# A decoder layer with expert retrieval on one core: one query-weight chunk kept on chip in place of two, and eleven places for gathered rows in place of ten

## Chip, cores, metric

The kernel runs on one core of a Trainium2 chip. The metric is the device time of one execution in microseconds (us). Of the kernel before there are three timed runs: 3097.0, 3091.28 and 3106.02 us, median 3097.0 us. Everything is float32.

## What is computed

The reference is one decoder layer over 1024 tokens of width 1024. Cut to what matters here:

```python
mix = hybrid_mixer(h, ...)      # x @ w_in; window attention and a gated DeltaNet; then @ w_out
h   = layer_norm(ALPHA * h + mix)
# PEER: product-key retrieval over 128*128 experts, in blocks of 128 tokens
q   = (xb @ w_query).reshape(L, 8, 2, 128)               # 2048 query columns
s   = einsum('lhpd,hpkd->lhpk', q, sub_keys)             # 16 lists of 128 scores
vals, idx = top_k(s, 16)                                 # for each list
best, pos = top_k(all 16*16 sums, 16); expert = ...      # 8 heads x 16 experts for a token
gate = softmax(best)
u, v = expert_u[expert], expert_v[expert]                # 1024 + 1024 numbers each
hid  = gelu(einsum('ld,lhkd->lhk', xb, u))
out  = einsum('lhk,lhkd->ld', hid * gate, v)
h    = layer_norm(ALPHA * h + out)
```

Each token draws 128 experts of its own and each expert is a row of 2048 numbers (u and v side by side), so the layer reads 1024 x 128 rows of 8 KB, 1073.7 MB, whatever is done about the weights.

## The kernel before, in words

The 1024 tokens are eight blocks (n = 0 to 7) of 128, one token in each partition. Two jobs are interleaved. The **mix** of block n is the projections, attention, DeltaNet, output projection, first norm, the queries of PEER and the choice of experts. The **experts** of block n are 128 slots: slot j is one gather of 128 rows (1 MB, an indirect DMA that POOL issues at L541), a dot product with the token's x on DVE (`experts`, L1849), a gelu and a gate on ACT (L1329 to L1336, which makes a small diagonal matrix `diag`), and four matmuls on PE that add the weighted v rows into `expert_sum` (L1007). While the mix of block n runs, the last slots of block n-1 are consumed. How much goes where is written out by hand: `EARLIER` and `OWN` (L146 to L158) give for each named step of the mix how many pairs of slots DVE, ACT and PE take after it. The steps of the choice of experts are `top0`, `more0`, `sel0`, `rest0`, `pick0` for the first two heads, then the same with 1, 2, 3. `pick0` writes the first 32 slots' indices (`expert_used`, L1799 and L1829) and raises `staged`. POOL waits for it (L533) before gather 0 of the new block. That moment is called the **turnover** here. Block n-1's slots 126 and 127 are dotted right after `pick0` (mark `pick0`, L1800), slots 124 and 125 after `rest0`, 122 and 123 after `sel0`. Then `turn_over` reads `expert_sum` on DVE (L1867) and copies x (L1838), and the steps from `top1` on keep DVE busy.

**The ring.** Gathered rows lie in `ring`, RING = 10 places of 8 KB per partition (1 MB each in all). `place(n, j)` is place (128 n + j) mod RING. POOL issues gather j when the slot RING before it has been added by PE:

```python
pool.wait_ge(*added.at(n, j - RING + 1))     # L536
gather(n, j)
```

**The weights.** `w_in`, `w_out` and `w_query` are cut into 23 chunks of 256 columns, 1 MB each: 0 to 10 for the input projection, 11 to 14 for the output projection, 15 to 22 for the queries. There are two staging buffers, `chunk0` and `chunk1`, each used as two halves of 512 KB. SP issues the loads in the order of use (`load`, L491 to L500). The load of a half waits until PE has used the half four loads earlier:

```python
sp.wait_ge(half_used, HALF_USED[last[0], last[1], last[2]])    # last = LOADS[g - 4]
alone(sp)
sp.dma_start(half_place(g), ...).then_inc(half_in[g % 4], 16)
```

The chunks in `KEPT`, 17 and 20 (the third and the sixth query chunk), are loaded once and stay in `kept` for all eight blocks; they are skipped at L523. So SP loads 4 + 6 chunks for the output projection and the queries of a block, and the input projection's chunks once for two blocks. The loads of x (`load_xT`, L505) stand behind the query chunks in SP's order, and behind them the chunks of the next blocks' input projection.

**The query phase on PE** (L952 to L987): `query_chunks(i)` multiplies chunks 15+2i and 16+2i, 32 matmuls each (L614), `score_keys(i)` makes four lists of scores (L967), and between them stand matmuls of pairs of slots of the block before: chunks 15, 16, scores, 17, 18, pair, scores, pair, 19, 20, pair, scores, pair, 21, 22, pair. PE takes a pair one pair later than DVE.

**Block 0.** Its weights are loaded ahead into the chunk buffers and the ring, which holds no rows yet: `EARLY` = 2 + RING places, used round (`early_place`, L446). The first gathers wait until PE has used the chunk in their place (L549).

Of the kernel before, what the change touches and what calls it, by code (L numbers as in the profile page):

```python
# [46 lines left out]
IN_CHUNKS = (HEADS * HD + 2 * KV * HD + 4 * DH * DK) // W  # L47
OUT_CHUNKS = D // W
Q_CHUNKS = LISTS * P // W
CHUNKS = IN_CHUNKS + OUT_CHUNKS + Q_CHUNKS  # L50
RING = 10
PAIRS = SLOTS // 2
SPAN = P // 2
PART = SLOTS // 4
DIAGS = 4
KEPT = (IN_CHUNKS + OUT_CHUNKS + 2, IN_CHUNKS + OUT_CHUNKS + 5)
STREAMED = [c for c in range(CHUNKS) if c not in KEPT]
EARLY = 2 + RING * 2 * D // (KT * W)

# [6 lines left out]
def in_pass(n):  # L66

    two = [m for m in (n + 1, n + 2) if m < NB]
    kinds = [(kind, two, PASS_BANKS[t]) for t, kind in enumerate(FLAT_KINDS if n % 2 else CONV_KINDS)] if two else []
    if n == 0:  # L70
        kinds += [(kind, [1], (b,)) for kind, b in zip(FLAT_KINDS, (5, 3, 4))]
    return kinds
# [7 lines left out]
def _use(c, blocks, streamed, halves=(0, 1)):  # L80
    for half in halves:
        if streamed:
            LOADS.append((c, blocks[-1], half))
    for m in blocks:
        for half in halves:
            HALF_USED[c, m, half] = len(HALF_USED) + 1
            if streamed:
                LOAD_OF[c, m, half] = len(LOADS) - len(halves) + halves.index(half)
# [6 lines left out]
for _n in range(NB):  # L95
# [4 lines left out]
    for _c in range(IN_CHUNKS + OUT_CHUNKS, CHUNKS):  # L100
        _use(_c, [_n], _n > 0 and _c not in KEPT)
    for _kind, _blocks, _ in in_pass(_n):
# [90 lines left out]
def build(nc, io):  # L193
    ctx = ExitStack()
    with ctx:
        def sb(name, cols, dt=F32, parts=P):
            return ctx.enter_context(nc.sbuf_tensor(name, [parts, cols], dt))

        def sem(name):
            return ctx.enter_context(nc.semaphore(name))  # L200

        def signal(name, per_block=1, before=0):
            return Signal(sem(name), per_block, before)
# [27 lines left out]
        chunk = [sb(f"chunk{i}", KT * W) for i in range(2)]  # L231
        ring = sb("ring", RING * 2 * D)
        kept = sb("kept", len(KEPT) * KT * W)

# [48 lines left out]
        late_in = sem("late_in")  # L283
        kept_in = [sem(f"kept_in{i}") for i in range(len(KEPT))]
        early_in = [sem(f"early_in{i}") for i in range(EARLY)]
# [86 lines left out]
        late_gates = signal("late_gates", 1)  # L372
        gathered = [sem(f"gathered{i}") for i in range(RING)]
        dotted = signal("dotted", SLOTS)
# [3 lines left out]
        diag_ready = signal("diag_ready", SLOTS)  # L378
        added = signal("added", SLOTS, before=RING)
        sums_read = signal("sums_read", 1, before=1)  # L380
# [18 lines left out]
        def place(n, j):  # L399

            r = (n * SLOTS + j) % RING
            return ring[:, r * 2 * D:(r + 1) * 2 * D]

        def arrived(n, j):

            return gathered[(n * SLOTS + j) % RING], 16 * ((n * SLOTS + j) // RING + 1)

# [34 lines left out]
        def kept_chunk(c):  # L442
            i = KEPT.index(c)
            return kept[:, i * KT * W:(i + 1) * KT * W]
# [29 lines left out]
        def _(sp):  # L474
# [5 lines left out]
            for c in range(1, CHUNKS):  # L480
                if c == IN_CHUNKS:
                    sp.dma_start(x1[:, :], io["x"][0]).then_inc(x_loaded.sem, 16)
                if c in KEPT:
                    sp.dma_start(kept_chunk(c), io["weights"][c]).then_inc(kept_in[KEPT.index(c)], 16)
# [1469 lines left out]
```

## Time and profile before

| | us |
|---|---|
| median of three runs (lowest, highest) | 3097.0 (3091.28, 3106.02) |
| profiled execution, its own time | 3092.87 |
| its span, first to last instruction | 3091.0 |
| PE busy in the span | 2352.3 (76%) |
| DVE busy | 2239.9 (72%) |
| POOL busy | 1195.2 (39%) |
| ACT busy | 1121.6 (36%) |
| data moved by the DMA engines | 1235.90 MB, mean 400 GB/s |

The profile is that of one execution, whose time is 4.1 us below the median. 1.9 us lie outside its span. Engines: PE is the matrix engine (PEld its weight loads), DVE the vector engine, ACT the scalar engine, POOL the engine that issues the gathers, SP the one that issues the weight loads. "DMA share" is the mean busy share of the 16 DMA engines. It reads up to 1.02 where they are all busy, so it can't tell full from nearly full, and GB/s beside it does. A line number is one of the code above.

### The profile page before, as it was taken

Reading aid. Unit: us, or ns where it says so; the run is one execution under the profiler, and the core shown is the slowest. Engines: PE = TensorE matmul, PEld = TensorE weight load, DVE = VectorE, ACT = ScalarE, POOL = GpSimd, SP = SyncE. Lnnn points to the kernel's source line nnn. Section 1 sums busy time; section 2 is a strip of 40 time slices with the busy share of each in tenths; the row PEclk is TensorE's granted clock in tenths of the full one; section 3 lists DMA queues with packets and bytes.
Section 4 is the critical chain, followed back from the end, with each engine's and each line's share of the span. In section 5 each row is a group of like instructions: output and inputs, shape, how many; then the busy total and the mean of one; then the engine's idle time right before and its main releaser. Section 6 shows DMA issues by size and latency. Waiting matters only on the chain.

```text
span 3091.0 us, 37872 instructions
## 1 busy us (share of the span) xinstructions
PE 2352.3 (76%) x11842; PEld 1330.6 (43%) x11842; DVE 2239.9 (72%) x5638; ACT 1121.6 (36%) x3530; POOL 1195.2 (39%) x1028
## 2 busy tenths in 40 slices
PE   8996878868788677877779778886778767785654
PEld 7773435424356343544346343542435434351111
DVE  5488656986679766897658966699657986678645
ACT  4123533254333533235322353224432363323222
POOL 0034452344423454234533345234443344434442
PEclk9998999989899898988989889988988889887777
DMA  8199999999999999999999999999999999999997
GB/s 350 42 383 412 420 421 406 412 413 420 420 408 418 417 420 420 397 407 419 420 419 404 416 420 421 407 399 413 420 420 404 418 418 420 420 372 421 410 421 323
DMA packets 189000, 1235.90 MB, mean 400 GB/s; under 512 B 21752, under 2 KB 21880, under 8 KB 54656
## 3 DMA queue, kind: packets, MB, share of 16 engines
q0 software_dynamic: 147456, 1073.81, 84.0%
q1 hardware_dynamic: 39168, 154.32, 12.7%
q10 hardware_dynamic: 2176, 5.36, 0.4%
q8 instruction: 95, 1.56, 0.2%
q14 instruction: 105, 0.86, 0.1%
HBM read 1229.21 MB, written 4.19 MB: 399 GB/s over the span
## 4 chain that ended last, share of the span: by engine, by line
DVE 32%; PE 29%; DMA 25%; ACT 6%; issue 5%; POOL 2%; DVEq 0%; POOLq 0%; SPq 0%; ACTq 0%
DMA ring<-in_uv,expert_used 24%; DVE ring L1849 14%; PE expert_sum L1007 13%; PE bank L614 7%; PE bank L621 2%; PE bank L603 2%; ACT diag L1336 2%; POOL ring L541 2%; DVE arena L1477 2%; DMA chunk<-in_weights 1%; DVE conv L1497 1%; DVE arena L1792 1%; DVE arena L1789 1%; DVE arena L1492 1%; DVE arena L1486 1%
## 5 line engine op out<-in xcount | busy, mean ns | idle before, releaser
L541 POOL DMA_INDIRECT ring<-in_uv,expert_used x1024 | 1195.0, 1167 | 1863.2 <-PE expert_sum L1007 1413.1
L1007 PE MATMUL expert_sum<-ring,diag 128*64 128x512 f32 x4096 | 1185.8, 708 | 639.1 <-ACT diag L1336 638.1
L1849 DVE CUSTOM_DVE_ANT_0 ring<-ring,x_pair 128x1024 f32<-128x1024 f32 x1024 | 1227.6, 1223 | 478.6 <-DMA ring<-in_uv,expert_used 472.8
L1007 PEld LDWEIGHTS expert_sum<-ring,diag 128*64 128x64 f32 x4096 | 312.3, 155 | 1261.0 <-issue 1246.4
L1329 ACT ACTIVATE h_raw<-h_raw 128x2 f32<-128x2 f32 x512 | 104.1, 203 | 1457.5 <-DVE h_raw L1849 1456.4
L1336 ACT ACTIVATE diag<-const,h_raw 128x64 f32<-128x64 f32 x1024 | 292.6, 332 | 4.9 <-PE expert_sum L1007 4.9
L1332 ACT ACTIVATE h_raw<-h_raw,gate_used 128x1 f32<-128x1 f32 x1024 | 245.6, 286 | 16.8
L614 PEld LDWEIGHTS bank<-oT,chunk 128*128 128x128 f32 x1344 | 152.7, 192 | 22.7 <-issue 22.7
L614 PE MATMUL bank<-oT,chunk 128*128 128x128 f32 x1344 | 158.6, 277 | 0.0
L1477 DVE MAX8 arena<-arena 128x8 f32<-128x128 f32 (+1 forms) x384 | 103.7, 325 | 32.6 <-ACT arena L1282 27.3
L603 PE MATMUL bank<-chunk,oT 128*128 128x256 f32 x464 | 110.0, 388 | 0.0
L603 PEld LDWEIGHTS bank<-chunk,oT 128*128 128x128 f32 x464 | 85.7, 191 | 41.1 <-issue 30.7
L614 PEld LDWEIGHTS bank<-o_cat,chunk 128*128 128x128 f32 x768 | 92.2, 200 | 21.2 <-issue 20.7
L621 PEld LDWEIGHTS bank<-arena 128*128 128x128 f32 x640 | 80.7, 202 | 41.4 <-issue 37.9
L614 PE MATMUL bank<-o_cat,chunk 128*128 128x128 f32 x768 | 96.8, 286 | 0.1
L1329 ACT ACT_TABLE_LOAD x74 | 94.9, 1283 | 5.2 <-DVE h_raw L1849 3.9
L621 PE MATMUL bank<-arena 128*128 128x128 f32 x640 | 90.5, 294 | 2.0 <-ACT arena L1236 0.6
L1849 DVE DVE_READ_ACCUMULATOR2_ANT h_raw<- 128x1 f32 x1024 | 83.9, 82 | 0.0
L1278 ACT COPY arena<-bank 128x512 f32<-128x512 f32 x32 | 18.7, 585 | 176.7 <-PE bank L614 176.7
L595 PE MATMUL bank<-chunk,o_cat 128*128 128x256 f32 x320 | 76.9, 392 | 7.2 <-DMA chunk<-in_weights 7.0
L1497 DVE SCALAR_TENSOR_TENSOR conv<-conv_in,conv_w,conv 128x128 f32<-128x128 f32 x288 | 77.8, 344 | 0.0
L614 PEld LDWEIGHTS bank<-xT_even,chunk 128*128 128x128 f32 x576 | 67.4, 196 | 13.7 <-issue 13.7
(276 smaller groups left out, 2621.6 us busy)
## 6 DMA issues: line engine op xcount, KB each, us to landing
chunk<-in_weights SPq DMA_DIRECT2D x228, 512.0 KB, 8.2
ring<-in_weights SPq DMA_DIRECT2D x17, 1024.0 KB, 23.9
ring<-in_uv,expert_used POOLq DMA_INDIRECT x1024, 15.5
chunk<-in_weights SPq DMA_DIRECT2D x4, 1024.0 KB, 20.4
x<-in_x SPq DMA_DIRECT2D x8, 512.0 KB, 14.6
out<-oT ACTq DMA_DIRECT2D x8, 512.0 KB, 9.2
o_cat<-in_xT SPq DMA_DIRECT2D x7, 512.0 KB, 14.6
xT_even<-in_xT SPq DMA_DIRECT2D x4, 512.0 KB, 10.0
```

The source lines that it names most:

```text
L541: pool.indirect_dma_start(out=place(n, j), out_offset=None, in_=io["uv"], in_offset=bass.IndirectOffsetOnAxis(ap=expert_used[:, j:j + 1], ...
L595: mm = pe.matmul(out, act[:, k, :], w[:, k % 4, :], start=(k == 0), stop=(k == KT - 1))
L603: mm = pe.matmul(out, act[:, k, :], w[:, k % 4, :], start=(k == ks[0]), stop=(k == ks[-1]))
L614: mm = pe.matmul(out, w[:, k % 4, i * P:(i + 1) * P], act[:, k, :], start=(k == 0), stop=(k == KT - 1))
L621: mm = pe.matmul(out[:, hs], lhsT[:, hs], rhs[:, hs], start=True, stop=True)
L1007: mm = pe.matmul(expert_sum[i][c * SPAN:(c + 1) * SPAN, :], diag[:, (j % DIAGS) * SPAN:(j % DIAGS + 1) * SPAN], place(n, j)[:, D + i * 512 ...
L1329: act.activation(h_raw[:, pair[0]:pair[1] + 1], h_raw[:, pair[0]:pair[1] + 1], ACT.Gelu).then_inc(gelued.sem, 1)
L1332: act.activation(h_raw[:, j:j + 1], h_raw[:, j:j + 1], ACT.Copy, scale=gate_used[:, j:j + 1]).then_inc(weighted.sem, 1)
L1336: act.activation(diag[:, (j % DIAGS) * SPAN:(j % DIAGS + 1) * SPAN], C["halves"], ACT.Copy, scale=h_raw[:, j:j + 1]).then_inc(diag_ready.s ...
L1477: ins = dve.max(values[:, one[part]], one[2])
L1497: stt(out=convo[:, t, :], in0=conv3[n % 2][:, t, k:k + P], scalar=conv_w[:, t * TAPS + k:t * TAPS + k + 1], in1=convo[:, t, :], op0=ALU.mu ...
L1849: dve.tensor_tensor_reduce(u, u, x_pair[:, (j % 2) * D:(j % 2 + 1) * D], 1.0, 0.0, ALU.mult, ALU.add, h_raw[:, j:j + 1]).then_inc(dotted.s ...
```

## The change

`KEPT` holds chunk 18 alone (the fourth query chunk). Chunks 17 and 20 are now streamed through the staging buffers for each block, and `kept` is half as large (8 KB less per partition). `RING` is 11, one place of 8 KB more per partition. `STREAMED` has 22 chunks in place of 21 and `EARLY` is 13 in place of 12. Nothing else in the file changes; the waits follow from these constants.

```diff
-RING = 10
+RING = 11
 PAIRS = SLOTS // 2
 SPAN = P // 2
 PART = SLOTS // 4
 DIAGS = 4
-KEPT = (IN_CHUNKS + OUT_CHUNKS + 2, IN_CHUNKS + OUT_CHUNKS + 5)
+KEPT = (IN_CHUNKS + OUT_CHUNKS + 3,)
 STREAMED = [c for c in range(CHUNKS) if c not in KEPT]
 EARLY = 2 + RING * 2 * D // (KT * W)
```

## Rows read from the trace of the kernel before

**Rows 1.** The page: GB/s in 40 slices of the span, and the two queues.

```profile
GB/s 350 42 383 412 420 421 406 412 413 420 420 408 418 417 420 420 397 407 419 420 419 404 416 420 421 407 399 413 420 420 404 418 418 420 420 372 421 410 421 323
...
q0 software_dynamic: 147456, 1073.81, 84.0%
q1 hardware_dynamic: 39168, 154.32, 12.7%
```

**Rows 2.** The page: the chain that ended last, by engine.

```profile
DVE 32%; PE 29%; DMA 25%; ACT 6%; issue 5%; POOL 2%; DVEq 0%; POOLq 0%; SPq 0%; ACTq 0%
```

**Rows 3.** Busy time by windows: stretch, its length, engines, granted clock, DMA share, GB/s.

```profile
664.00:860.00 196.00, 149.66 (x675) 74.61 (x676) 128.40 (x244) 85.29 (x268) 89.02 (x75) 0.86 1.01 420
176.00:3072.00 2896.00, 2191.01 (x10799) 1196.18 (x10799) 2138.04 (x5342) 1061.40 (x3401) 1181.92 (x1013) 0.88 1.01 414
```

**Rows 4.** The same view: the seven turnovers, blocks 1 to 7.

```profile
536.00:546.00 10.00, 7.74 (x30) 3.09 (x26) 6.82 (x19) 2.76 (x7) 6.63 (x7) 0.97 0.91 322
900.00:912.00 12.00, 11.37 (x63) 6.63 (x61) 8.75 (x22) 3.75 (x10) 6.07 (x7) 1.00 0.95 352
1264.00:1280.00 16.00, 13.87 (x96) 9.81 (x93) 10.05 (x29) 6.17 (x15) 4.26 (x5) 1.00 0.88 315
1640.00:1650.00 10.00, 9.69 (x37) 3.94 (x35) 6.87 (x16) 3.50 (x8) 7.03 (x8) 0.89 0.97 349
2002.00:2014.00 12.00, 10.89 (x84) 8.97 (x86) 9.55 (x28) 6.17 (x15) 2.90 (x3) 1.00 0.87 292
2376.00:2384.00 8.00, 7.68 (x43) 4.17 (x42) 4.71 (x14) 3.50 (x8) 4.91 (x5) 1.00 0.90 311
2738.00:2750.00 12.00, 11.68 (x89) 8.95 (x87) 9.53 (x28) 6.17 (x15) 2.85 (x3) 1.00 0.36 133
```

**Rows 5.** DVE in order of time at block 2's turnover: start, length, idle before.

```profile
896.26 1.22 DVE L1849 CUSTOM_DVE_ANT_0 ring<-ring,x_pair 128x1024 f32<-128x1024 f32 x1 [3.52 <-DMA ring<-in_uv,expert_used]
...
902.48 0.72 DVE L1829 CAST expert_used<-arena 64x16 uint32<-64x16 f32 x4
```

**Rows 6.** POOL in order of time, same turnover.

```profile
883.49 0.93 POOL L541 DMA_INDIRECT ring<-in_uv,expert_used  x1 [0.30 <-issue]
904.10 1.17 POOL L541 DMA_INDIRECT ring<-in_uv,expert_used  x1 [19.68 <-DVE expert_used L1829]
```

**Rows 7.** PE and SP in order of time, same turnover: chunks 17, 19, 21 and 22, loads.

```profile
871.65 3.84 PE L614 MATMUL bank<-oT,kept 128*128 128x128 f32 x32
883.82 3.84 PE L614 MATMUL bank<-oT,chunk 128*128 128x128 f32 x32
895.98 7.41 PE L614 MATMUL bank<-oT,chunk 128*128 128x128 f32 x64
...
861.59 26.49 SPq L500 DMA_DIRECT2D chunk<-in_weights  x8
```

**Rows 8.** DMA of 860 to 896 us: its queues, and the chunk loads to landing.

```profile
q0 software_dynamic: 1510, 11.01, 73.9%
q1 hardware_dynamic: 1077, 3.95, 27.3%
...
chunk<-in_weights SPq DMA_DIRECT2D x8, 512.0 KB, 9.1
```

**Rows 9.** Source line 500 over the whole span: its loads to landing.

```profile
DMA to landing us min/median/max: 3.8/8.2/12.9
```

**Rows 10.** By windows again: dips outside the turnovers.

```profile
256.00:272.00 16.00, 10.41 (x47) 4.61 (x47) 13.21 (x43) 10.59 (x28) 6.80 (x6) 1.00 0.97 386
596.00:668.00 72.00, 52.62 (x211) 26.81 (x211) 69.84 (x206) 25.93 (x84) 28.85 (x25) 0.84 1.00 407
1328.00:1400.00 72.00, 54.39 (x230) 28.83 (x228) 69.56 (x205) 26.21 (x84) 29.62 (x26) 0.87 1.01 407
2060.00:2144.00 84.00, 65.91 (x278) 35.01 (x274) 81.38 (x242) 29.70 (x99) 33.81 (x30) 0.87 1.00 402
2912.00:2924.00 12.00, 12.00 (x33) 3.63 (x33) 5.75 (x11) 2.54 (x10) 3.09 (x5) 0.62 0.88 344
```

## The prediction

> **What bounds the kernel now.** I read the 40 slices and the queues first. From the sixth slice on the core moves 397 to 422 GB/s in every slice but three, and the gathers' queue alone takes 84.0% of the 16 DMA engines' time, the weights' queue 12.7% [rows 1]. No compute engine comes near that: PE is at 76%, DVE at 72%. The chain of waits seems to say otherwise, DVE 32%, PE 29%, DMA 25% [rows 2], but it follows semaphores, and a gather that queues behind others is late because of bytes, whoever issued it. So the deciding view is busy time by windows. Between 664 and 860 us the DMA moves 420 GB/s without a break; I take 420 as full. From 176 to 3072 us it averages 414 [rows 3], which is 2896 x 6/420 = 41 us short of full. Time is therefore bytes over 420, plus at most those 41 us, plus the start and the tail, which the change hardly touches. The question is how many bytes come on top, and whether they fall into the 41 us.
>
> Where do the 41 us lie? Mostly at the seven turnovers [rows 4]. Their shortfalls against 420, window by window, are 2.3, 1.9, 4.0, 1.7, 3.7, 2.1 and 8.2 us, together 23.9. The mechanism is in DVE's and POOL's order of time. Slot 125's row is there at 896.26, DVE then runs the index work of pick0 and writes the indices at 902.48 [rows 5], and POOL, which has issued the last gather of the old block at 883.49, sits 19.68 us and issues the next at 904.10 [rows 6]. From 896 the DMA has only slots 126 and 127 and some weights left. A second group of dips lies where DVE is 96 to 98% busy with the choice of experts, and at one place in block 7 where PE is held up [rows 10]: 1.3, 2.2, 2.2, 3.6 and 2.2 us, 11.5 together. There the ring is full of rows that nobody has consumed yet.
>
> **Bytes added.** One more chunk is streamed in blocks 1 to 7: 7 x 2 halves of 0.524 MB = 7.34 MB. Price: the weights' queue moved 154.32 MB in 12.7% of 3091 us, 393 GB/s [rows 1]. That gives **+18.7 us** if nothing hides it. Startup is even: 23 chunks are loaded once before and after, and 13 early places with 1 kept chunk hold as many as 12 with 2. The one kept load less and one ring load more cancel. SP's 14 added issues cost nothing: SP has no other work, and in the phase in question it waits for PE.
>
> The Trainium skill, page DMA: Bandwidth & Descriptors, section Bandwidth, measured 341 GB/s for a 1 MB transfer against 425 for 16 MB, and gives as a rule to batch to 1 MB and more. At that page's 341 the added bytes would be 21.5 us, an estimate. The trace doesn't agree for this kernel, since with both queues at work it moves 414 to 417.
>
> **Where the bytes fall.** SP is paced by PE: a half is loaded when the half four loads back is used. Before, from 861.59, SP loads 18, 19, 21, 22 and then x. After, it loads 17, 19, 20, 21, 22 and then x, with 22 issued when PE has used chunk 20 (some 890.3 to 891.2) and not chunk 19 (886.6 to 887.5). Everything behind it moves back by 3.7 us, towards or into the gap that opens at 896. Two bounds. Above, all bytes go ahead of slot 125 and nothing is hidden, 0 us. Below, each turnover swallows what it has room for, at most one chunk's 2.67 us (18.7/7): 2.3 + 1.9 + 2.67 + 1.7 + 2.67 + 2.1 + 2.67 = 16.0 us. Which is nearer? From 860 to 896 the weights' queue got 27.3% of the DMA, 3.95 MB or 110 GB/s [rows 8], with loads outstanding nearly all the time. The new order wants 3.67 MB in the 34.4 us up to 896, 107 GB/s. So the queue already moved about what the new order asks of it, little is taken from the gathers, and the excess slides behind slot 125. I take two thirds of 16.0: **-10.7 us**.
>
> By the Trainium skill, same page, section Queues, rings and completion order, each DMA engine round-robins between the queues that have work, a packet from each. By that rule the weights' share isn't changed by how deep either queue is, and nearly all 16.0 us would be hidden. A share near 27% fits it, but no row here has the deeper queue.
>
> **The eleventh place.** POOL may run one gather further ahead, 1.05 MB or 2.5 us of DMA work. Where the DMA is full anyway this is worth nothing. Before pick0 it is worth nothing either, as the gathers' queue isn't empty there. It counts where the DMA runs dry because the ring is full, once a block: after a turnover POOL issues 11 gathers in a burst and not 10, and DVE starts its long busy stretch with 2.5 us more in stock. Each dip can give back at most 2.5 us: 1.3 + 2.2 + 2.2 + 2.5 + 2.2 = 10.4 [rows 10]. Below that, an odd ring splits the pairs: PE frees two places at a time, and only the even slot of a pair is asked for a pair earlier. Bounds 0 and 10.4; I take **-6.5 us**. If the dips are really DVE being late, the place moves the DMA's idle time rather than removing it.
>
> **Waits on PE.** Chunk 17 was on chip; now its first half is issued at 861.59 and wanted at 871.65 [rows 7], 10.1 us later, against 9.1 us to landing in this phase [rows 8]. Chunk 21, issued at about 886.6 and wanted at 895.98, has 9.4; chunk 22, issued at 890.3 and wanted at 899.7, has 9.4. All three are covered by under 1.1 us, and the longest landing in the trace is 12.9 [rows 9]. Queued behind a late chunk on PE are the pairs of slots, the scores, and the last pair of the block, for which DVE's turn_over waits; then top1 and all of DVE's busy stretch start late, and there DVE has no slack. Bounds: 0, and 12.9 - 9.4 = 3.5 us in each of seven turnovers, 24.5. I take half a microsecond in each: **+3.5 us**.
>
> Chunk 18, now kept, leaves an equal pause in SP's order where 17 and 20 had theirs. DVE, ACT and the arithmetic are unchanged.
>
> **Sum.** 18.7 - 10.7 - 6.5 + 3.5 = +5.0 us. On the profiled execution's 3092.9 that is 3097.9; that execution lies 4.1 us below the median of the three, so against the median it is 3102. I write 3100.
>
> **Rivals.** A change under 0.5%, 15.5 us, can hardly be told from none here.
>
> *All hidden.* The gaps take 16.0, the place gives 10.4, PE never waits: 18.7 - 26.4 = -7.7, 3085 on the profiled time, 3089 on the median. For it speak the 107 against 110 GB/s. Against it, two turnovers have room for under 2 us. Chance 0.2. To go past -15.5 the kernel would have to lose 34 of its 41 us of shortfall while it moves more bytes: 3077. Only a ring that shrinks the turnover gap itself does that, by slot 125 being there earlier. Its gather has 22 us between issue and arrival, all of it queueing, so issuing it earlier brings it no earlier. Chance 0.06.
>
> *Bytes in full.* The weights push slot 125 back, pick0 with it, and the gap is as wide as before: 18.7 less a few us of the ring, 3109 to 3116. For it speaks that the DMA is full up to 896, so what is added before that has to displace something. Chance 0.14.
>
> *PE starved of chunks 17, 21 and 22.* On the slower side, and it decides once a half takes longer than the 10.1 or 9.4 us it has. Five chunks in a row on a queue that gets 110 GB/s need 5.24/110 = 47.6 us, and 22 is wanted after 39. If 3.5 us are lost at each turnover and DVE's busy stretch passes them on: 18.7 - 10.7 - 6.5 + 24.5 = +26, 3119 to 3123. Against it: from 896 on the gathers are nearly done and the weights have the DMA for themselves. Chance 0.12.
>
> That the change doesn't do what it says is no rival: 8 KB per partition go from one buffer to the other, and both constants are used throughout.
>
> **The numbers.** The forecast (partly hidden, 3092 to 3108) has 0.48. Faster by over 0.5%: 0.06. Slower by over 0.5% (above 3112.5): 0.12 from the starved PE and a bit over half of "bytes in full", 0.08, so 0.20. Within 0.5%: 0.74. The range reaches down to the all-hidden case, 3083, and up to the starved one, 3121.
>
> **What would show it.** Bytes 7.34 MB more, at 242 chunk loads in place of 228. The seven turnover windows nearer to 420 GB/s than in [rows 4], with block 7's 8.2 us cut by some 2.5. The dips of [rows 10] shallower. PE's waits for chunks in the query phase under a microsecond each. POOL's burst after a turnover with 11 gathers. It is wrong if slot 125 arrives 2.5 us later after chunk 15 than now with the turnover windows unchanged, if L614 waits for chunks by several us at each turnover, or if the dips of the DVE-bound stretches stay as deep as they are.

## The result and the profile after

The changed kernel takes 3126.7 us in the median of six runs (3120.6 to 3135.1), the one before 3099.5 us beside it. The ratio is 1.0086, interval 1.0072 to 1.0100: 27 us slower, 22 to 31, where 5 were forecast and 3121 was the upper end. The experiments come in four later sets, each taken together on one chip with the kernel before beside it: e1 to e4, e5 to e8, e9 to e12, e13 to e15. The changed kernel, run again in three of them, gave 24.5, 13.3 and 29.7 us. The sign is sure, the size is one of 13 to 30 us, and what makes it vary is part of the findings. All costs below are (ratio - 1) x 3097 us; two executions far off all others, 4467 us in e2 and 3494 us of the kernel before beside e1 to e4, are left out of the ratios.

The page of the changed kernel, its GB/s in 40 slices, its queues, and from its costliest groups the query matmuls and the reading of the sums; it answers to [rows 1]. Its span is 3118.7 us; this execution, of 3120.56 us, was the fastest of the six, so the profile shows 27.7 us more than before.

```profile
GB/s 347 41 394 415 420 420 399 406 415 410 420 414 398 418 414 420 402 408 415 421 419 406 417 413 421 412 393 413 420 420 407 405 417 420 420 374 419 421 421 311
...
q0 software_dynamic: 147456, 1073.81, 83.5%
q1 hardware_dynamic: 41184, 161.66, 13.1%
...
L614 PE MATMUL bank<-oT,chunk 128*128 128x128 f32 x1568 | 198.3, 286 | 27.7 <-DMA chunk<-in_weights 27.6
L614 PEld LDWEIGHTS bank<-oT,chunk 128*128 128x128 f32 x1568 | 187.1, 198 | 60.5 <-DMA chunk<-in_weights 32.9
...
L1867 DVE SCALAR_TENSOR_TENSOR oT<-x_pair,expert_sum 64x512 f32<-64x512 f32 x32 | 21.9, 685 | 85.5 <-remote 42.9
```

The bytes are as foreseen: the weights' queue has 161.66 - 154.32 = 7.34 MB more, in 242 chunk loads, for 0.4% more of the engines' time. What is new stands in the last three rows. PE, which before waited 0.4 us in all for chunks at L614, waits 27.6 us, 3.9 at each turnover. And DVE waits 85.5 us for the sums at L1867 over its eight readings, where it waited 24.6. ("Remote" is the profile's word for a releaser that it couldn't name; the program has one core, and the wait at that line is for PE.)

DVE and then POOL in order of time, changed kernel, the turnover of block 2, as [rows 5, 6]:

```profile
905.30 0.72 DVE L1829 CAST expert_used<-arena 64x16 uint32<-64x16 f32 x4
...
924.10 1.39 DVE L1867 SCALAR_TENSOR_TENSOR oT<-x_pair,expert_sum 64x512 f32<-64x512 f32 x2 [15.14 <-PE expert_sum L1007]
```

```profile
906.93 1.17 POOL L541 DMA_INDIRECT ring<-in_uv,expert_used  x1 [16.55 <-DVE expert_used L1829]
...
914.62 0.94 POOL L541 DMA_INDIRECT ring<-in_uv,expert_used  x1 [0.30 <-issue]
918.02 0.94 POOL L541 DMA_INDIRECT ring<-in_uv,expert_used  x1 [2.46 <-PE expert_sum L1007]
```

From the indices to the reading of the sums 18.8 us pass; before it was 6.6 (902.48 to 909.07):

```profile
909.07 2.78 DVE L1867 SCALAR_TENSOR_TENSOR oT<-x_pair,expert_sum 64x512 f32<-64x512 f32 x4 [2.93 <-PE expert_sum L1007]
```

POOL's burst, which was to be eleven gathers long, stops after seven, because the places wait for PE. The reason is in PE's order of time over the same stretch, as [rows 7]:

```profile
875.61 1.16 PE L614 MATMUL bank<-oT,chunk 128*128 128x128 f32 x8
878.62 4.57 PE L614 MATMUL bank<-oT,chunk 128*128 128x128 f32 x24 [1.85 <-DMA chunk<-in_weights]
883.01 3.75 PE L614 MATMUL bank<-oT,kept 128*128 128x128 f32 x32
...
903.68 1.16 PE L614 MATMUL bank<-oT,chunk 128*128 128x128 f32 x8
906.69 8.15 PE L614 MATMUL bank<-oT,chunk 128*128 128x128 f32 x56 [1.85 <-DMA chunk<-in_weights]
```

PE starts chunk 17 with the half that is there, and stands still until the second half lands; the same at chunk 21. And there is a second loss: the 24 records after the first stop take 4.57 us where 32 on the kept chunk take 3.75. The windows show why; columns are length, engines, granted clock, DMA share, GB/s. First the changed kernel, then the same kernel in e9:

```profile
878.00:883.00 5.00, 4.38 (x24) 4.38 (x25) 4.47 (x18) 0.00 (x0) 0.66 (x1) 0.66 1.00 411
...
907.00:915.00 8.00, 8.00 (x58) 7.84 (x58) 1.89 (x7) 0.00 (x0) 6.17 (x7) 0.79 1.00 395
```

```profile
875.50:879.00 3.50, 3.14 (x28) 3.14 (x29) 2.72 (x7) 0.00 (x0) 0.76 (x1) 1.00 1.00 411
...
903.00:907.00 4.00, 3.18 (x28) 2.99 (x28) 3.83 (x12) 0.00 (x0) 0.34 (x1) 1.00 0.81 293
```

PE had stood still for 1.85 us each time, and then the granted clock was 0.66 over 5 us: part of them at the lower of its two levels, 1.2 GHz, where in the kernel before it was 1.00, that is 2.4 GHz, from 864 to 909. In e9 PE stood still at the same two places, for 1.5 and 2.3 us, and the clock stayed at 1.00; the 24 records after the first stop took 2.94 us. So the fall doesn't follow from the length of one stop, and what decides it these rows don't show.

**Where the DMA's shortfall went.** The prediction's account was bytes plus shortfall. The shortfall against 420 GB/s in us, summed over windows of 2 us (one above 420 counts against it), for three parts of each block counted from the reading of the sums (R): turnover, R - 20 to R + 15; busy stretch, R + 15 to R + 130; the rest.

| kernel | turnovers | busy stretches | rest |
|---|---|---|---|
| before | 26.6 | 10.8 | 0.4 |
| changed | 19.5 | 24.0 | 4.9 |
| e9, changed | 30.0 | 8.8 | 0.5 |
| e13, changed | 19.0 | 24.3 | 8.1 |
| e2, bytes at the turnover | 11.6 | 27.3 | 0.4 |
| e4, third staging buffer | 13.6 | 22.4 | 0.6 |
| e3, idle matmuls | 38.3 | 35.9 | 0.7 |
| e7, twelve places alone | 35.9 | 1.0 | 0.3 |
| e8, nine places, three chunks kept | 37.2 | 44.2 | 5.6 |

In the first set and in e13 the turnovers did fill, as foreseen, and what was filled there opened again in the busy stretch behind it. In e9 neither happened: the same kernel had 30.0 us at the turnovers, more than the kernel before, and 8.8 behind them. The busy stretches of blocks 1 and 2, windows of the kernel before and of the changed one:

```profile
557.00:672.00 115.00, 88.92 (x378) 49.27 (x374) 111.07 (x338) 39.74 (x134) 42.83 (x38) 0.89 1.01 412
924.00:1039.00 115.00, 90.51 (x536) 56.81 (x532) 109.56 (x333) 39.03 (x129) 40.87 (x38) 0.89 1.01 417
```

```profile
564.00:679.00 115.00, 86.83 (x378) 48.63 (x375) 111.17 (x339) 39.82 (x135) 42.68 (x39) 0.90 1.01 406
939.00:1054.00 115.00, 88.02 (x538) 55.98 (x536) 110.87 (x336) 40.56 (x133) 42.51 (x39) 0.92 1.00 404
```

### The profile page after: what moved, and what is told of

It is laid out like the page before. It is cut to its first block, busy times and chain, and to the rows that moved or that the text cites. A ratio compares the mean times of both kernels' runs of the same rounds, so it can differ in the third digit from the quotient of the medians.

```text
span 3118.7 us, 37900 instructions
## 1 busy us (share of the span) xinstructions
PE 2354.9 (76%) x11842; PEld 1333.6 (43%) x11842; DVE 2233.6 (72%) x5638; ACT 1121.8 (36%) x3530; POOL 1202.6 (39%) x1028
## 3 DMA queue, kind: packets, MB, share of 16 engines
q1 hardware_dynamic: 41184, 161.66, 13.1%
## 4 chain that ended last, share of the span: by engine, by line
DVE 35%; DMA 26%; PE 23%; ACT 6%; issue 6%; another core or an unknown queue 3%; POOL 1%; DVEq 0%; POOLq 0%; SPq 0%; ACTq 0%
DMA ring<-in_uv,expert_used 22%; DVE ring L1849 15%; PE expert_sum L1007 10%; PE bank L614 5%; DMA chunk<-in_weights 4%; DVE arena L1477 2%; ACT diag L1336 2%; PE bank L603 2%; PE bank L621 1%; DVE arena L1492 1%; DVE conv L1497 1%; DVE arena L1486 1%; DVE arena L1484 1%; POOL ring L541 1%
## 5 line engine op out<-in xcount | busy, mean ns | idle before, releaser
L1007 PE MATMUL expert_sum<-ring,diag 128*64 128x512 f32 x4096 | 1180.5, 705 | 626.4 <-ACT diag L1336 624.4
L1007 PEld LDWEIGHTS expert_sum<-ring,diag 128*64 128x64 f32 x4096 | 311.6, 154 | 1244.5 <-issue 1229.8
L1332 ACT ACTIVATE h_raw<-h_raw,gate_used 128x1 f32<-128x1 f32 x1024 | 245.7, 287 | 16.8
L614 PE MATMUL bank<-oT,chunk 128*128 128x128 f32 x1568 | 198.3, 286 | 27.7 <-DMA chunk<-in_weights 27.6
L614 PEld LDWEIGHTS bank<-oT,chunk 128*128 128x128 f32 x1568 | 187.1, 198 | 60.5 <-DMA chunk<-in_weights 32.9
L1477 DVE MAX8 arena<-arena 128x8 f32<-128x128 f32 (+1 forms) x384 | 103.8, 326 | 28.1 <-ACT arena L1282 22.8
L614 PEld LDWEIGHTS bank<-o_cat,chunk 128*128 128x128 f32 x768 | 95.2, 205 | 21.5 <-issue 21.0
L1278 ACT COPY arena<-bank 128x512 f32<-128x512 f32 x32 | 18.8, 586 | 235.3 <-PE bank L614 203.5
L614 PE MATMUL bank<-o_cat,chunk 128*128 128x128 f32 x768 | 99.8, 291 | 0.2
L1867 DVE SCALAR_TENSOR_TENSOR oT<-x_pair,expert_sum 64x512 f32<-64x512 f32 x32 | 21.9, 685 | 85.5 <-remote 42.9
```

The costliest lines, as they stand in the source:

```text
L614: mm = pe.matmul(out, w[:, k % 4, i * P:(i + 1) * P], act[:, k, :], start=(k == 0), stop=(k == KT - 1))
L1007: mm = pe.matmul(expert_sum[i][c * SPAN:(c + 1) * SPAN, :], diag[:, (j % DIAGS) * SPAN:(j % DIAGS + 1) * SPAN], place(n, j)[:, D + i * 512 ...
L1332: act.activation(h_raw[:, j:j + 1], h_raw[:, j:j + 1], ACT.Copy, scale=gate_used[:, j:j + 1]).then_inc(weighted.sem, 1)
L1477: ins = dve.max(values[:, one[part]], one[2])
```

## The experiments

**e1, e10, e14: chunk 18 kept, ring of ten.** The change without its second half, called the twin below:

```diff
-RING = 11
+RING = 10
```

> The change without the eleventh place: chunk 18 kept, ring of ten. The changed kernel is 27 us over the one before. Theory A (the 7.34 MB cost their full 18.7 us, and PE, which waits for chunks 17, 21 and 22, makes the rest, the place being worth little): 25 to 30 us over before. Theory B (the place gives back its 6.5 us and hides a dearer streaming): 32 to 38 us over before. Theory C (the odd ring of eleven, with its split pairs, does harm by itself): under 22 us over before.

Measured: 1.0057 (1.0038 to 1.0077), 17.7 us, less than the 26.6 that the changed kernel had shown and the 24.5 of e5. Theory C had asked for that. That looked as if the eleventh place did harm. It had to be tried side by side, and was, below.

**e2 and e12: the bytes alone.** Ring of ten and both chunks kept as before, but chunk 17 is loaded again into its own place for every block. In e2 behind the loads of x, at the turnover; in e12 ahead of `rows_staged`, in the stretch where the DMA is full.

```diff
+                sp.wait_ge(*used(AGAIN, n))          # AGAIN = KEPT[0]
+                alone(sp)
+                sp.dma_start(kept_chunk(AGAIN), io["weights"][AGAIN]).then_inc(...)
...
-                    if m == 0:
-                        pe.wait_ge(kept_in[KEPT.index(c)], 16)
+                    if m == 0 or c == AGAIN:
+                        pe.wait_ge(kept_in[KEPT.index(c)], 16 * (m + 1))
```

> The kernel before, with chunk 17 loaded again into its own kept place for every block, issued behind the loads of x at the turnover, so the same 7.34 MB go where the DMA has its gap, and no chunk is wanted sooner than before. Theory A (bytes cost in full wherever they go because the DMA is full): 16 to 20 us over before, PE's waits for chunks unchanged. Theory D (the gap swallows what is put into it, and the changed kernel only failed because its bytes lie ahead of the gap and PE waits for them): 2 to 8 us over before, with the seven turnover windows near 420 GB/s.

> As the bytes at the turnover (14.6 us over before), but chunk 17 is loaded again behind the input projection's chunks and ahead of x, in the stretch where the DMA moves 420 GB/s. Theory A in full: 16 to 19 us over before. If the gap at the turnover did hide some 4 us there, this one is 2 to 5 us slower than that one; if the two are equal, where the bytes lie doesn't matter at all.

Measured: e2 1.0047 (1.0034 to 1.0059), 14.6 us; e12 1.0066 (1.0046 to 1.0086), 20.4 us. The price of 18.7 us for the bytes in full fits e12, whose interval is 14 to 27 us. The gap would have hidden some 6 us, but the intervals overlap and e2 and e12 are of different sets, so this is not shown. In e2 the turnover windows were near 420, as the theory of the gap asked: block 2's rose from 395 to 417. But its cost was not 2 to 8 us, and its busy stretches show the reason. First the kernel before at its turnover of block 2, then e2 there and in the busy stretch behind it:

```profile
889.00:924.00 35.00, 28.08 (x176) 18.87 (x177) 27.23 (x85) 11.09 (x29) 10.04 (x10) 0.96 0.99 395
```

```profile
892.00:927.00 35.00, 28.02 (x176) 18.83 (x177) 27.25 (x85) 11.04 (x29) 10.05 (x10) 0.95 1.02 417
...
927.00:1042.00 115.00, 89.69 (x528) 56.24 (x526) 106.64 (x326) 38.98 (x128) 38.75 (x36) 0.87 1.00 408
```

**e3: PE late, no bytes.** Idle matmuls ahead of chunks 17 and 21 in the kernel before:

```diff
+                        if n and c in (2, 6):
+                            for _ in range(4):
+                                pe.matmul(b[:, :], ident, const[:, 0:512], start=True, stop=True)
```

> The kernel before with four idle 128x512 matmuls ahead of chunk 17 and four ahead of chunk 21 in blocks 1 to 7, some 1.9 us each, so PE is some 3.7 us later at each turnover with no byte added; that is about what PE waits for chunks in the changed kernel (27.6 us in all for L614). Theory A (PE's lateness is the part over 18.7 us): 6 to 12 us over before. Theory E (each us of lateness is passed on in full through DVE's busy stretch): 22 to 28 us over before. Theory F (PE's lateness is absorbed): 0 to 3 us.

Measured: 1.0110 (1.0084 to 1.0136), 34 us. The delay was mis-sized: the four take 3.54 us a time and not 1.9, as PE's order of time in e3 shows, so 7.1 us at each turnover and 49.6 in all.

```profile
880.92 3.70 PE L961 MATMUL bank<-const 128*128 128x512 f32 x8
884.46 3.73 PE L614 MATMUL bank<-oT,kept 128*128 128x128 f32 x32
```

34/49.6 = 0.69 of the lateness reaches the end (0.52 to 0.85 by the interval), without one byte more. PE's order in this phase is on the path of a kernel whose DMA looks full. The absolute numbers of theory A and E can't be held against it because of the wrong size; by the share, E is nearer than A, and F is out.

**e4: a third staging buffer**, with chunk 18 kept and a ring of ten:

```diff
-        chunk = [sb(f"chunk{i}", KT * W) for i in range(2)]
-        half_in = [sem(f"half_in{i}") for i in range(4)]
+        chunk = [sb(f"chunk{i}", KT * W) for i in range(3)]
+        half_in = [sem(f"half_in{i}") for i in range(6)]
...
-                if g > 3:
-                    last = LOADS[g - 4]
+                if g > 5:
+                    last = LOADS[g - 6]
```

> Chunk 18 kept, ring of ten, and the 8 KB spent on a third staging buffer, so that six halves and not four can be loaded ahead and no query chunk is late. Theory A (18.7 us of bytes plus PE's waits): 15 to 20 us over before, PE's wait for chunks at L614 near nothing. Theory D (what costs is only being late): within 6 us of before. If PE's waits don't matter: as e1_kept18_ring10.

Measured: 1.0033 (1.0019 to 1.0048), 10.2 us (6 to 15), 7.5 under the twin e1 of the same set, and no execution of the one overlaps with the other (3104.5 to 3111.4 against 3115.6 to 3119.8). No wait for chunks at L614 is left, and DVE's wait for the sums is back at its old size (waits of e4):

```profile
DVE oT L1867 <- PE expert_sum L1007: 25.6, 8, 5.0
```

So the same bytes, streamed in the same phase, cost 10.2 us when PE need not wait for them. That is a little below the 15 to 20 of theory A: some 8 of the 18.7 us are hidden.

**e6 and e7: the places alone.** Chunks 17 and 20 are not streamed and not kept: their weights are taken from `sub_keys`, so queries, experts and output are other numbers, and 2 MB of loads at the start are left out. RING is 11 in e6 and 12 in e7.

```diff
-            return kept[:, i * KT * W:(i + 1) * KT * W]
+            return sub_keys[:, :]
```

> The eleventh place alone: chunks 17 and 20 are not streamed, both are taken from the 8 KB of sub_keys (their queries are then other numbers, and other experts are chosen), so the bytes and the waits for weights are those of before (2 MB of kept loads less at the start). Theory G (the place is a small gain, as forecast): 3 to 8 us faster than before. Theory H (an odd ring, or more gathers queued ahead of the weights, does harm): 3 to 10 us slower, with PE's and DVE's waits grown. Theory I (the place is worth nothing, since PE's order sets the turnover): within 2 us.

> As the eleventh place alone, with twelve places, an even ring. Theory G: 6 to 12 us faster than before. Theory H by the odd ring: the harm is gone and it is at or below before; theory H by depth: twice the harm of eleven. Theory I: within 2 us.

Measured: e6 0.9995 (0.9984 to 1.0006), e7 0.9990 (0.9981 to 0.9999): -1.5 us (-5 to +2) and -3 us (-6 to 0). e6 is theory I; e7 is a little over its 2 us, and both runs also load 2 MB less at the start. So a place by itself is worth at most a few us, and the odd ring does no harm by itself. And yet the twelfth place did to the dips what the eleventh was forecast to do, as e7's windows show, the busy stretches of blocks 1 and 2 and then the turnover of block 2:

```profile
561.00:676.00 115.00, 88.16 (x378) 49.03 (x376) 111.17 (x338) 39.71 (x134) 42.27 (x39) 0.89 1.02 419
928.00:1043.00 115.00, 90.04 (x536) 56.52 (x532) 109.28 (x330) 38.71 (x127) 41.50 (x38) 0.88 1.02 419
...
892.00:928.00 36.00, 29.06 (x183) 19.51 (x183) 28.24 (x89) 11.52 (x31) 11.93 (x12) 0.95 0.96 378
```

The busy stretches are full, 1.0 us of shortfall in place of 10.8, and the turnovers have 9.3 us more of it. The idle time moved and didn't go.

**e8: the change turned round**, nine places, chunks 17, 20 and 21 kept, 7.34 MB less.

> The change turned round: nine places, and chunks 17, 20 and 21 kept, so 7.34 MB less. Theory A with a place worth nothing: 15 to 19 us faster than before. If a place is worth 6 us or more of stock in DVE's busy stretch: 6 to 12 us faster, with deeper dips there. Theory H by depth: more than 18 us faster.

Measured: 1.0087 (1.0072 to 1.0101), 27 us slower, where every theory had it faster. The long window shows 407 GB/s where [rows 3] has 414:

```profile
176.00:3072.00 2896.00, 2198.21 (x10768) 1202.93 (x10769) 2123.24 (x5316) 1052.93 (x3366) 1162.46 (x1006) 0.87 0.99 407
```

Ten places are at a knee: going from ten to nine cost 27 us although 7.34 MB fell away, going from ten to eleven with the same bytes gave 1.5 (e6). Whether depth or the odd number hurts at nine wasn't tried apart; at eleven the odd number did not hurt.

**e5, e9, e13: the changed kernel again, beside the others.**

> The changed kernel once more, beside the ring experiments. In its profile DVE waits 10 to 15 us for PE at L1867 in each turnover, against 7 to 9 with a ring of ten. All theories: 24 to 30 us over before. If it comes out within 3 us of the 17.8 us that chunk 18 kept with a ring of ten costs (4 runs), the eleventh place does nothing by itself; if it stays above 24 us, the place costs some 7 us.

> The changed kernel a third time, side by side with its twin with ten places. The eleventh place alone was worth 0.2 us. Theory I (a place is worth nothing): both within 3 us of each other, some 18 to 25 us over before. Theory J (the place does harm once PE waits for weights, since DVE and POOL run further ahead and the gathers keep the DMA from the weights): the changed kernel 5 to 9 us over its twin, PE's waits for chunks longer in it.

> The twin: chunk 18 kept, ring of ten. Theory I: as the changed kernel, 18 to 25 us over before. Theory J: 16 to 19 us over before, 5 to 9 under the changed kernel.

> The changed kernel, side by side with its twin on one chip once more. If the eleventh place is worth nothing on the whole and the three calls differ by chip or by how the queues fall into step: 13 to 27 us over before, and the difference to the twin between -9 and 9, no steadier sign than before. If the place gains: 5 to 9 us under the twin again.

> The twin with ten places: 17 to 22 us over before, as in two calls already.

Measured: e5 1.0079 (1.0066 to 1.0091), 24.5 us, just over the 24 above which the place was to be the culprit. Side by side it is not: e9 1.0043 (1.0027 to 1.0059) against e10 1.0069 (1.0053 to 1.0085); e13 1.0096 (1.0077 to 1.0115) against e14 1.0120 (1.0102 to 1.0139). Both sets had the same chip, and both kernels moved up together from one to the next, by 16 us, while the kernel before stayed within 1.3 us. So e14, at 37.2 us, missed its 17 to 22 by far. The difference between the two held: the changed kernel is 8.1 and 7.4 us faster than its twin with ten places (8.7 and 9.0 by the medians). The harm that e1 hinted at came of comparing across sets, and theory J is out, and theory I (within 3 us) with it. Once PE is late, the eleventh place is worth some 8 us. That is as much as the third staging buffer gave over the same twin in e4, 7.5 us, for the same 8 KB; no set has the two side by side.

**e11 and e15: another chunk kept.** `KEPT` is chunk 21 in e11 and chunk 17 in e15, eleven places in both.

> The changed kernel with chunk 21 kept in place of chunk 18, so PE's last two chunks, 21 and 22, are there when wanted, and only 17 comes late; bytes and places are the same. Theory A (bytes 12 to 15 us, the rest is PE's lateness): PE's wait for chunks at L614 falls from 27 us to half, and the time lies 4 to 8 us under the changed kernel. If the lateness costs nothing and only bytes do: the same time.

> Chunk 17 kept in place of 18, eleven places. Its wait goes; 20, 21 and 22 are then each loaded one step ahead. If the cost over the bytes goes with PE's waits (0.6 to 0.7 us for each us, as the idle matmuls and chunk 21 kept say): waits at L614 of 15 to 30 us and 20 to 30 us over before, in the order of the waits of e13, e14 and this one. If it goes with something else: no such order.

Measured: e11 1.0125 (1.0104 to 1.0145), 38.7 us; e15 1.0097 (1.0081 to 1.0112), 30 us. e11 missed in the direction: it was to be 4 to 8 us faster than the changed kernel and was 25 us slower than e9 of the same set. e15 ended level with e13 beside it, at the upper end of its 20 to 30 us, and the order that it asked for, cost by waits, did not come. In PE's order of time at the turnover of block 2, e11 waits for 17, 18 and 20, now that the chunks from 15 to 20 are all streamed one after the other; its waits are the longest of all:

```profile
PE bank L614 <- DMA chunk<-in_weights: 45.6, 28, 4.0
```

But waits for chunks alone don't order the runs: e13 waited 22.8 us and cost 29.7, e9 waited 26.9 and cost 13.3. What does so better among the kernels with late chunks, though roughly, is the length of the whole query phase on PE, from its first matmul on chunk 15 to the reading of the sums, mean of the seven turnovers of the profiled execution:

| kernel | phase, us | waits at L614, us | cost, us |
|---|---|---|---|
| before | 50.9 | 0.4 | 0 |
| e6, eleven places alone | 51.1 | 0 | -1.5 |
| e7, twelve places alone | 51.2 | 0 | -3 |
| e8, nine places | 50.6 | 0 | 27 |
| e12, bytes midway | 51.4 | 0 | 20.4 |
| e4, third buffer | 51.9 | 0 | 10.2 |
| e2, bytes at the turnover | 52.1 | 0 | 14.6 |
| e1 and e10, the twin | 55.1, 55.5 | 25.6, 25.2 | 17.7, 21.4 |
| e9, changed | 55.4 | 26.9 | 13.3 |
| e3, idle matmuls | 57.1 | 0 | 34 |
| e14, the twin | 57.2 | 24.8 | 37.2 |
| e5, changed | 57.3 | 27.1 | 24.5 |
| e15, chunk 17 kept | 58.5 | 30.1 | 30.0 |
| changed, first and e13 | 58.9, 59.0 | 27.6, 22.8 | 26.6, 29.7 |
| e11, chunk 21 kept | 59.9 | 45.6 | 38.7 |

e8 and e12 show that the phase isn't all: their costs have other causes. e14 doesn't fit well either.

The changed kernel's phase is 8.0 us longer than before, 56 us over the seven, and its traces say where that lies. Waits at L614 are 27.6 us. The lower clock took 10.7 us, reckoned as the length of each phase times what its granted clock lacked to 1.00. And 12.4 us lie between the end of PE's last record at L1007 and DVE's reading. In the kernel before that is 0.15 us each time, and here it is 3.6, 3.4, 2.3 and 3.7 in blocks 1, 5, 6 and 7. The remaining 5 us are not pinned down. This is block 7 of the changed kernel, PE and then DVE:

```profile
2777.77 1.94 PE L1007 MATMUL expert_sum<-ring,diag 128*64 128x512 f32 x8 [0.32 <-ACT diag L1336]
```

```profile
2783.39 2.78 DVE L1867 SCALAR_TENSOR_TENSOR oT<-x_pair,expert_sum 64x512 f32<-64x512 f32 x4 [10.23 <-remote]
```

DVE waits there for the adds alone, so they ended later than their records do, whose ends are modelled. Why, no row shows. In e9, with nearly the same waits (26.9), the clock took 1.7 us and this last part nothing, and the phase was 55.4. In e13 the two were 14.3 and 9.8 us. Between e9 and the first set the phases differ by 25 us, of which the clock makes 9 and the unexplained part 12. So the clock is at most a part of what makes the change dear in one set and cheap in another; no run held it fixed, and the rest is open.

## Why the prediction was wrong

**Bytes.** Priced right: 18.7 us in full, 20.4 measured (e12, 14 to 27). The net of 8.0 after hiding is a little under the 10.2 and 14.6 of e4 and e2, so 4 to 8 us were hidden and not 10.7. The gap did swallow bytes, block 7's shortfall fell from 8.2 to 5.6 us by this row of the changed kernel, the 2.6 that was forecast:

```profile
2764.00:2776.00 12.00, 9.65 (x74) 7.93 (x72) 8.82 (x28) 4.12 (x9) 3.96 (x4) 1.00 0.59 224
```

**The eleventh place.** Forecast -6.5 on the ground that it closes the dips. Alone it is -1.5 (-5 to +2), and in the changed kernel, beside its twin, -8. So the size came out near by accident. The reason given was wrong: e7, with two places more, closed the dips and gained 3 us. The prediction's own doubt, that the place moves the DMA's idle time, was right.

**Waits on PE.** This is the step that failed: "I take half a microsecond in each: +3.5 us". It is a term mis-sized, and a chain cut short. Margins of 0.3 to 1.0 us between a median landing and the need were taken as cover, though the longest landing stood in [rows 9] at 12.9. Halves landed later with one chunk more asked for: in e9 the median was 10.8 us and the longest 16.8. The prediction held that the queue already moved what the new order wants, 107 against 110 GB/s. Over 36 us from the same point of the phase, 864 to 900, the changed kernel's weights got less than before, 96 GB/s, while both queues together moved 418:

```profile
q1 hardware_dynamic: 940, 3.46, 23.9%
```

PE then waited 3.9 us at each turnover, where 0.5 was forecast: 27.6 us in place of 3.5. Its phase grew by 8.0, and DVE waited some 8.5 us more for the sums each time. The prediction had named this as its sign of being wrong, several us at L614 at each turnover. What it costs was measured with ten places alone, e1 against e4 where it is gone: 7.5 us. The changed kernel's 26.6 lie 16 us over e4, but across sets, so that size stays open.

**The rival that came.** "PE starved of chunks 17, 21 and 22", with +26 us and a chance of 0.12. Its place was right and its size near the 26.6 of the first set, though its sum counts 10.7 us hidden, which the runs don't bear out, and no loss on PE beyond the waits. Against it I had set that the weights would have the DMA to themselves from 896 on; the first stop, at chunk 17, lies 20 us ahead of that, and the second one at its edge.

**The frame.** "Time is bytes over 420 plus at most 41 us" is true as arithmetic and misled as a cause. The sum of the shortfalls is 37.8, 39.3, 36.6 and 37.2 us in four kernels that end between 3094 and 3113 (before, e2, e4, e7), however it is spread: filled at one end, it opened at the other. So in the profiled executions of e2 and e4 the added bytes, 7.34 MB at 420 or 17.5 us, were paid almost in full; the profiled execution of the kernel before lies 4 us under its median, which is why the medians show less. In the changed kernel the sum is 48.4, and 17.5 + 10.6 = 28.1 us are its 27.7. e3 shows that not bytes alone set the time: with no byte more the shortfall went from 37.8 to 74.9 us. The reading that fits is that PE and then DVE set the time of the turnover and of the busy stretch, and the DMA's idle time there is a remainder; apart from e3 that is argued.

**Readings.** Three small ones in the prediction were off and change nothing: between 256 and 272 us DVE is 83% busy, not 96 to 98% [rows 10]; from the sixth slice on two lie under 397 GB/s, not three; and from 861.59 to 899.7 are 38 us, not 39.

## What to carry to other kernels

A DMA that moves close to its full rate in nearly every slice doesn't mean that nothing else is on the path: look at what each stretch waits for at its end, and don't take the small shortfall for room before a run has filled it. Where a load gets less lead than the longest landing in the trace, count it as late, and count with it what stands behind it on its engine, the clock included. Which weight stays resident matters as well: chunk 21 in place of 18 cost 25 us more (e11 beside e9), chunk 17 in place of 18 nothing (e15 beside e13). Spare memory for more stock of something that isn't short gives next to nothing (e6); behind a late stream, a third staging buffer and an eleventh place gave about the same.

## What the runs showed that was not expected

The same change cost 13.3 us in one set and 29.7 in another on one chip, its twin 21.4 and 37.2, while the kernel before moved by 1.3 us. So a few per mille between two kernels of this kind can only be read side by side. Nine places in place of ten cost 27 us though 7.34 MB fell away. And a stop of PE of 1.85 us was followed by 5 us at a granted clock of 0.66 in one execution, while in another, stops of 1.5 and 2.3 us at the same places were followed by none. Last, the reading of the sums came up to 3.7 us after the end of the last add record in the changed kernel (4.3 in e15), against 0.15 in the kernel before, and no row says why.
